# Mixers: the recurrence is prepared beside attention's end, its tree rows get the split input's space, branch products stand in the norm's waits, three barriers go

## The chip, the cores and the metric

One core of a Trainium2 chip runs the whole program as one launch. The metric is the device time of that launch in microseconds (us), the median of the executions. All arithmetic is float32. The products against the token mixers' wide inputs are split into a high and a low part.

## What is computed

The reference runs two blocks on 256 tokens of width 1024. The change concerns the first block, which has two layers. In each, a token mixer stands between two gated feed-forward parts:

```python
def token_mixer(h, w_in, pool_w, pool_scale, rel_bias, lb, norm_g, w_branch, w_out):
    proj = h @ w_in
    (a, q, k, v, qi, ki, wi, hq, hf, hi, hg, gates) = jnp.split(proj, MIX_SPLITS, axis=-1)
    y_a = pool_mixer(a, pool_w, pool_scale)
    y_b = sparse_attention(q, k, v, qi, ki, wi, rel_bias)      # top 64 of 256 keys, 4 heads
    y_c = hgrn2(hq, hf, hi, hg, lb, norm_g)                    # gated recurrence, 4 heads, then an RMS norm
    g = jax.nn.sigmoid(gates.reshape(B, S, 3, D_MODEL))
    merged = (g[:, :, 0] * (y_a @ w_branch[:256]) + g[:, :, 1] * (y_b @ w_branch[256:512])
              + g[:, :, 2] * (y_c @ w_branch[512:]))
    return merged @ w_out
```

The recurrence `hgrn2` is computed as a binary tree over tokens: for each of eight levels the prefix and suffix sums of the log decays (`pref`, `suff`) are exponentiated, multiplied with keys and queries into `treeX`, and multiplied with each other on TensorE.

## The kernel before

Every engine has its own program, written out by hand, and semaphores join them. Weights stream from memory as panels of 1 MB (256 output columns) into four slots (`slots`). SyncE issues them in order: the load of panel p waits until the panel four places before it has been multiplied. Products of a panel go to one of four banks (`accs`), and `acc_open` waits until the bank's last user was read. Four more banks (`mix`) hold everything small. Where a phase is named in `CARRY`, VectorE also weighs a 1 MB panel of another part in each step (`cond_weigh`), and SyncE waits for `cond_done` before it loads the next of these. In the branch phase of layer 0 there are three, in layer 1 none; in the output phase (`mixout`) four in either layer, those of layer 1 with twice the work.

A mixer runs in this order: 15 input panels; the pool; attention, with gate panels 2 to 6 in TensorE's waits; the recurrence (`hgrn`), with gate panels 7 to 11 in its waits; the branch products, 4 panels u in three parts r each (`ymix` rows 0-1 pool, 2-3 attention, 4-7 recurrence), whose results VectorE multiplies with the gates and adds into `merged`; and `mixout`, 4 panels that multiply `merged`. Between the phases stands a barrier of TensorE, VectorE and ScalarE:

```python
        def stage_end(eng, count):
            count[0] += 1
            eng.drain().then_inc(stage, 1)
            eng.wait_ge(stage, 3 * count[0])
```

Names: `hg_key` says that the keys and the first `pref` are made, `hg_x` that a level's rows are ready, `hg_mm` that its products are done, `hg_o` that the recurrence's output stands in `mix`, `hg_sq` that ScalarE squared it, `hg_ms` that TensorE summed the squares, `hg_inverse` that the inverse roots are there, which TensorE then spreads (`spread`) for the last product of VectorE into `ymix[:, 4:8]`. `probT_ready` and `attn_mm` belong to attention: transposed probabilities copied out, and the product with the values done.

Space: the scratch region at `TMP` is shared. Attention's `logit` lies in `TMP + 2816` and on, over the `treeX` and `pairs` of the recurrence. `sums` (the tensor `decay_sums`, 4 rows of 1024) holds the split input (`mix_hi`, `mix_lo`) during the 15 input panels and nothing from then on until the second block.

In the profile, L678 is a gate or mixout panel (32 matmul records a panel; one float32 matmul is two records), L923 the transposes, L933 the product with the values, L957 to L966 the tree's products, L975 to L977 the output's, L982 the sums of squares, L853 the spread, L1358 the branch products, L480 the barrier. L76, L81, L86, L91, L96 and L116 are the helpers that record every ScalarE and VectorE operation, L2144 a weighing.

## Time and profile before

| | |
|---|---|
| median of 3 executions | 2945.57 us (2941.25 to 2946.78) |
| the profiled execution | 2941.72 us, of which the span is 2939.7 us |
| TensorE busy | 2711.7 us, 92% of the span |
| VectorE, ScalarE, GpSimd busy | 1943.9, 1091.0, 238.7 us |
| granted TensorE clock, mean | 0.977 |
| memory read | 465.58 MB, 159 GB/s over the span |

TensorE is close to always busy, so what counts are the stretches where it waits or where its granted clock is below 1. All times below are microseconds from the span's start. The mixer of layer 0 ends its input panels near 351, and that of layer 1 near 1078.

### The profile page before, as it was taken

How to read it: one execution, taken by the hardware profiler on the slowest of the kernel's cores; microseconds unless marked ns; L12 is line 12 of the kernel's file. 1: busy time of each engine (PE TensorE's matmuls, PEld its weight loads, DVE VectorE, ACT ScalarE, POOL GpSimd, SP SyncE). 2: the span in 40 equal slices, each digit the busy share in tenths (PEclk: the TensorE clock that was granted, in tenths of full speed). 3: DMA queues.
4: the chain of work that ended last, by engine and by line, in shares of the span. 5: the costliest groups of instructions: out<-in, count | busy, mean ns of one | idle time of the engine just before them, and what ended most of it. 6: DMA issues, size and time to landing. Idle time of an engine off the chain costs nothing.

```text
span 2939.7 us, 48614 instructions
## 1 busy us (share of the span) xinstructions
PE 2711.7 (92%) x18294; PEld 2306.4 (78%) x18294; DVE 1943.9 (66%) x3303; ACT 1091.0 (37%) x1389; POOL 238.7 (8%) x135
## 2 busy tenths in 40 slices
PE   3999998999999999999989978999999899889998
PEld 3998977899998887799967854687744777667887
DVE  6776665777777766476746473577787676664881
ACT  2434432443542433154464542433300644542211
POOL 0000000000000000000012300244300000000000
PEclk9999999999999999999999989999999999999999
DMA  8775734677575553345512200222277221113442
GB/s 309 271 289 220 263 113 178 219 275 287 214 272 226 193 192 104 130 172 211 204 61 78 81 21 29 72 94 92 107 266 292 76 73 67 58 58 127 146 169 74
DMA packets 106384, 469.15 MB, mean 160 GB/s; under 512 B 7052, under 2 KB 57304, under 8 KB 58328
## 3 DMA queue, kind: packets, MB, share of 16 engines
q1 hardware_dynamic: 106200, 466.67, 43.8%
q8 instruction: 119, 1.95, 0.3%
q14 instruction: 65, 0.53, 0.1%
HBM read 465.58 MB, written 1.06 MB: 159 GB/s over the span
## 4 chain that ended last, share of the span: by engine, by line
PE 31%; DVE 12%; DVEq 7%; ACT 3%; issue 3%; DMA 2%; ACTq 1%; SPq 0%
DVEq L2859 4%; PE accs L830 4%; PE accs L693 3%; PE accs L678 3%; PE accs L694 3%; PE accs L695 3%; DVE arena L2836 3%; PE accs L1225 2%; PE accs L1226 2%; PE accs L1227 2%; DVE arena L2144 1%; DMA cond_panel<-wc 1%; PE accs L1358 1%; ACT arena L76 1%; DMA arena<-wc 1%
## 5 line engine op out<-in xcount | busy, mean ns | idle before, releaser
L693 PE MATMUL accs<-normed_r,arena_r 128*128 128x256 f32 (+2 forms) x1864 | 585.5, 314 | 17.2 <-DVEq L2189 6.3
L694 PE MATMUL accs<-arena_r 128*128 128x256 f32 x2069 | 585.8, 283 | 0.0
L695 PE MATMUL accs<-normed_r,panel_r 128*128 128x256 f32 (+2 forms) x1872 | 584.7, 312 | 0.0
L86 DVE TENSOR_TENSOR panel_r<-panel,arena_r 128x1024 fp32r<-128x1024 f32 (+1 forms) x295 | 390.6, 1324 | 162.7 <-ACTq L1507 117.7
L1506 ACT ACTIVATE arena_r<-panel 128x1024 fp32r<-128x1024 f32 (+1 forms) x292 | 330.5, 1132 | 328.8 <-DMA panel<-w 138.8
L693 PEld LDWEIGHTS accs<-normed_r,arena_r 128*128 128x128 f32 (+1 forms) x1864 | 350.4, 188 | 54.2 <-issue 14.0
L694 PEld LDWEIGHTS accs<-arena_r 128*128 128x128 f32 x2069 | 390.9, 189 | 1.1 <-issue 0.2
L695 PEld LDWEIGHTS accs<-normed_r,panel_r 128*128 128x128 f32 (+1 forms) x1872 | 350.2, 187 | 23.9 <-issue 0.8
L678 PE MATMUL accs<-normed,panel 128*128 128x256 f32 x1536 | 344.3, 384 | 6.7 <-ACTq L480 3.0
L2836 DVE SCALAR_TENSOR_TENSOR arena<-accs,vectors,arena 128x189 f32<-128x189 f32 (+2 forms) x704 | 279.3, 428 | 95.3 <-issue 65.4
L678 PEld LDWEIGHTS accs<-normed,panel 128*128 128x128 f32 x1536 | 291.7, 192 | 54.1 <-issue 4.6
L830 PE MATMUL accs<-arena,panel 128*128 128x256 f32 (+1 forms) x832 | 255.5, 469 | 2.0 <-DVEq L2744 0.8
L830 PEld LDWEIGHTS accs<-arena,panel 128*128 128x128 f32 x832 | 157.8, 190 | 99.2 <-issue 86.8
L76 ACT ACTIVATE arena<-accs 128x512 f32<-128x512 f32 (+2 forms) x128 | 75.3, 588 | 370.4 <-PE accs L695 232.4
L693 PE MATMUL accs<-arena_r 128*128 128x256 f32 x704 | 201.2, 286 | 10.7 <-DVEq L2189 10.7
L695 PE MATMUL accs<-arena_r,panel_r 128*128 128x256 f32 x704 | 199.7, 284 | 0.0
L1435 POOL TENSOR_TENSOR panel_r<-panel,arena_r 128x1024 fp32r<-128x1024 f32 x70 | 169.0, 2414 | 333.9 <-ACTq L1514 333.0
L76 ACT ACTIVATE arena<-arena 128x512 f32<-128x512 f32 (+7 forms) x108 | 97.5, 903 | 161.0 <-DVEq L2782 58.6
L1513 ACT ACTIVATE arena_r<-panel 128x1024 fp32r<-128x1024 f32 x72 | 76.3, 1060 | 204.0 <-PE accs L695 188.3
L91 DVE SCALAR_TENSOR_TENSOR residual<-accs,mods,residual 128x256 f32<-128x256 f32 x96 | 46.4, 483 | 156.0 <-PE accs L830 76.0
L76 ACT ACTIVATE arena<-residual 128x512 f32<-128x512 f32 (+1 forms) x56 | 31.9, 569 | 317.0 <-DVEq L2889 268.9
L693 PEld LDWEIGHTS accs<-arena_r 128*128 128x128 f32 x704 | 134.8, 192 | 12.5 <-issue 7.0
(417 smaller groups left out, 4714.6 us busy)
## 6 DMA issues: line engine op xcount, KB each, us to landing
panel<-w SPq DMA_DIRECT2D x250, 1024.0 KB, 4.9
panel<-w SPq DMA_DIRECT2D x48, 1408.0 KB, 8.0
cond_panel<-wc SPq DMA_DIRECT2D x57, 1024.0 KB, 6.3
normed<-wc SPq DMA_DIRECT2D x43, 1024.0 KB, 6.5
arena<-wc SPq DMA_DIRECT2D x19, 1024.0 KB, 4.9
residual<-xs SPq DMA_DIRECT2D x2, 1024.0 KB, 9.7
residual<-wc SPq DMA_DIRECT2D x1, 1024.0 KB, 12.0
residual<-crows SPq DMA_DIRECT2D x2, 512.0 KB, 9.4
```

What stands on the lines that cost most here:

```text
L76: i = self.eng.activation(*a, **k)
L86: i = self.eng.tensor_tensor(*a, **k)
L678: mm = pe.matmul(acc[b][:, o:o + ntok], w[:, k * PANEL + j * P:k * PANEL + j * P + P], rhs(k), start=(k == 0), stop=(k == KD - 1))
L693: pe.matmul(out, hi[:, k, 0:m], src_hi(k), start=clear and k == 0, stop=False, skip_group_check=True)
L694: pe.matmul(out, hi[:, k, 0:m], src_lo(k), start=False, stop=False, skip_group_check=True)
L695: mm = pe.matmul(out, lo[:, k, 0:m], src_hi(k), start=False, stop=last and k == n - 1, skip_group_check=True)
L830: mm = pe.matmul(acc[a % BANKS][:, o:o + ntok], w[:, k * PANEL + j * P:k * PANEL + j * P + P], src(part * kper + k), start=first, stop=(pa ...
L1435: pool.tensor_tensor(lo, half_panel(g, u, j), hi, ALU.subtract)
L1506: act.eng.activation(split_parts(g, u, j)[0], half_panel(g, u, j), ACT.Copy)
L1513: act.eng.activation(split_parts(g, u, j)[0], half_panel(g, u, j), ACT.Copy)
L2836: dve.eng.scalar_tensor_tensor(out=out, in0=src, scalar=scale, in1=out, op0=ALU.mult, op1=ALU.add)
L2859: dve.drain()
```

## The change

- The tree's rows (`pref`, `suff`, `treeX`) move from the scratch region to `sums`, so they no longer overlap attention's `logit`.
- The barriers between attention and recurrence, recurrence and branch, and branch and mixout go. Their place is taken by waits on `attn_mm` (VectorE, before the memset of `pairs`, which still overlaps attention's space), `ymix_early` and `ymix_late` (TensorE, for the attention rows and the recurrence rows of `ymix`) and `merged` (TensorE, before each second k of mixout's first panel).
- Gate panel 7 moves ahead of attention's product with the values, gate panel 11 ahead of the recurrence's output products.
- ScalarE's copy of attention's result moves from the end of attention to behind the first level's exponentials, together with the read of gate panel 7.
- Three of the twelve branch parts are multiplied earlier: (0,0) before the sums of squares, (0,1) behind them, (1,0) behind the spread.

```diff
-        pref, suff = region(TMP, 4 * T), region(TMP + 1024, 4 * T)
-        treeX = [region(TMP + 2048 + 1024 * i, 4 * T) for i in range(2)]
+        pref, suff = sums[:, 0, :], sums[:, 1, :]
+        treeX = [sums[:, 2 + i, :] for i in range(2)]
...
+                        if merge is not None and j == 0 and k % 2 == 0:
+                            pe.wait_ge(S("merged"), 4 * merge + k // 2 + 1)
...
                     mm.then_inc(S("probT_mm"), 1)
-                    if qb == 0:
-                        gate(l, 6)
+                    gate(l, 6 + qb)
...
             def hgrn(l):
                 k4, q4 = kk, qf
-                gate(l, 7)
...
+                gate(l, 11)
                 pe.wait_ge(S("hg_acc"), 7 * l + 7)
                 pe.wait_ge(S("hg_pairs"), l + 1)
...
                 mm.then_inc(S("hg_o"), 1)
-                gate(l, 11)
+                pe.wait_ge(S("ymix_early"), l + 1)
+                branch_part(l, 0, 0)
                 pe.wait_ge(S("hg_sq"), l + 1)
...
                 mm.then_inc(S("hg_ms"), 1)
+                branch_part(l, 0, 1)
                 pe.wait_ge(S("hg_inverse"), l + 1)
                 spread(0, 8).then_inc(S("hg_spread"), 1)
+                branch_part(l, 1, 0)
...
+            def branch_part(l, u, r):
+
+                g = G[f"branch{l}"]
+                ks = (range(0, 2), range(2, 4), range(4, 8))[r]
+                w = panel_in(g, 0, u)
+                b = acc_open(g, 0, u, r)
+                for j in range(2):
+                    for k in ks:
+                        mm = pe.matmul(acc[b][:, j * T:j * T + T], w[:, k * PANEL + j * P:k * PANEL + j * P + P],
+                                       ymix[:, k, :], start=(k == ks[0]), stop=(k == ks[-1]))
+                mm.then_inc(ready[b], 1)
...
                         attention(l)
-                        stage_end(pe, count)
                         hgrn(l)
-                        stage_end(pe, count)
-                        g = G[f"branch{l}"]
+                        pe.wait_ge(S("ymix_late"), l + 1)
                         for u in range(4):
...
+                            for r in range(3):
+                                if (u, r) not in ((0, 0), (0, 1), (1, 0)):
+                                    branch_part(l, u, r)
                         g = G[f"mixout{l}"]
                         for u in range(4):
-                            features(g, 0, u, lambda k: merged[:, k, :], T)
+                            features(g, 0, u, lambda k: merged[:, k, :], T, merge=l if u == 0 else None)
...
-                act.wait_ge(S("attn_mm"), l + 1)
-                act.activation(ymix[:, 2:4, :].rearrange("p a b -> p (a b)"), mix[:, 1, :], ACT.Copy)
...
-                    if lv in (1, 3, 5):
+                    if lv == 0:
+                        gate(l, 7)
+                        act.wait_ge(S("attn_mm"), l + 1)
+                        act.activation(ymix[:, 2:4, :].rearrange("p a b -> p (a b)"), mix[:, 1, :], ACT.Copy).then_inc(S("ymix_early"), 1)
+                    if lv in (3, 5):
                         gate(l, 7 + lv // 2)
...
-                dve.memset(pairs[:, :, :], 0.0)
...
+                    if lv == 0:
+                        dve.wait_ge(S("attn_mm"), l + 1)
+                        dve.memset(pairs[:, :, :], 0.0)
...
-                            dve.tensor_tensor(dst, dst, mtmp[:, :, :], ALU.add)
+                            i = dve.tensor_tensor(dst, dst, mtmp[:, :, :], ALU.add)
+                            if r == 2:
+                                i.then_inc(S("merged"), 1)
```

TensorE's program at attention's end, before (layer 0; L678 with `panel0` is gate panel 7):

```order
L923 MATMUL mix<-constants,arena 128x128 [waits prob_ready]
L923 MATMUL mix<-constants,arena 128x128 x7
L933 MATMUL mix<-arena 64x128 [waits probT_ready]
L933 MATMUL mix<-arena 64x128 x3
L933 MATMUL mix<-arena 64x128 [waits probT_ready]
L933 MATMUL mix<-arena 64x128 x7
L678 MATMUL accs<-normed,panel0 128x256 [waits acc_free0,panel_landed0,stage_end]
L678 MATMUL accs<-normed,panel0 128x256 x15
L957 MATMUL mix<-arena 32x32 [waits hg_key]
```

The same place now (the gate panel's line is L680, the product with the values L934):

```order
L925 MATMUL mix<-constants,arena 128x128 [waits prob_ready]
L925 MATMUL mix<-constants,arena 128x128 x7
L680 MATMUL accs<-normed,panel0 128x256 [waits acc_free0,panel_landed0]
L680 MATMUL accs<-normed,panel0 128x256 x15
L934 MATMUL mix<-arena 64x128 [waits probT_ready]
L934 MATMUL mix<-arena 64x128 x3
L934 MATMUL mix<-arena 64x128 [waits probT_ready]
L934 MATMUL mix<-arena 64x128 x7
L957 MATMUL mix<-arena 32x32 [waits hg_key]
```

The gate panel stands ahead of the product with the values, and no barrier is left between them and the tree.

TensorE's program between the recurrence's output and the branch products, before (layer 0):

```order
L678 MATMUL accs<-normed,panel0 128x256 [waits acc_free0,panel_landed0]
L678 MATMUL accs<-normed,panel0 128x256 x15
L982 MATMUL mix<-ones_h,arena 128x1 [waits hg_sq]
L982 MATMUL mix<-ones_h,arena 128x1 x7
L853 MATMUL mix<-constants,rms_columns 128x128 [waits hg_inverse]
L853 MATMUL mix<-constants,rms_columns 128x128 x7
L1358 MATMUL accs<-arena,panel1 128x256 [waits acc_free1,panel_landed1,stage_end]
L1358 MATMUL accs<-arena,panel1 128x256 x3
```

The same place now (L999 is `branch_part`):

```order
L999 MATMUL accs<-arena,panel1 128x256 [waits acc_free1,panel_landed1,ymix_early]
L999 MATMUL accs<-arena,panel1 128x256 x3
L984 MATMUL mix<-ones_h,arena 128x1 [waits hg_sq]
L984 MATMUL mix<-ones_h,arena 128x1 x7
L999 MATMUL accs<-arena,panel1 128x256 [waits acc_free2,panel_landed1]
L999 MATMUL accs<-arena,panel1 128x256 x3
L855 MATMUL mix<-constants,rms_columns 128x128 [waits hg_inverse]
L855 MATMUL mix<-constants,rms_columns 128x128 x7
L999 MATMUL accs<-arena,panel2 128x256 [waits acc_free0,panel_landed2]
L999 MATMUL accs<-arena,panel2 128x256 x3
L999 MATMUL accs<-arena,panel1 128x256 [waits acc_free3,panel_landed1,ymix_late]
```

Gate panel 11 has left this place (it now stands ahead of the output products), and three branch parts have come in between the three steps of the norm.

ScalarE's program from the end of attention to the second level, now (before, the copy `arena<-mix 128x512` stood ahead of the table load, and the table load waited for `hg_key`):

```order
L76 ACTIVATE arena<-mix 128x1024 [waits probT_mm]
L76 ACT_TABLE_LOAD
L76 ACTIVATE decay_sums<-decay_sums,constants 128x1024 [waits hg_key]
L76 ACT_TABLE_LOAD
L76 ACTIVATE decay_sums<-decay_sums 128x512 [waits hg_zero]
L76 ACTIVATE decay_sums<-decay_sums 128x512
L76 ACTIVATE arena<-accs 128x512 [waits acc_ready0]
L76 ACTIVATE arena<-mix 128x512 [waits attn_mm]
L76 ACTIVATE decay_sums<-decay_sums 128x256x2 [waits hg_sums]
```

The logarithm and the first exponentials stand directly behind the copy of the transposed probabilities; the read of gate panel 7 and the copy of attention's result stand behind them, ahead of the second level.

## Rows read from the trace of the kernel before

**Rows 1.** Timeline at attention's end, layer 0: start, duration, engine, line [idle before <-releaser]

```profile
410.76 1.04 PE L923 MATMUL mix<-constants,arena 128*128 128x128 f32 x8
...
411.83 1.02 ACT L76 ACTIVATE arena<-mix 128x1024 f32<-128x1024 f32 x1 [0.28 <-PE mix L923]
...
412.91 1.58 PE L933 MATMUL mix<-arena 128*64 128x128 f32 x16 [0.52 <-ACT arena L76]
...
415.23 1.65 DVE L81 TENSOR_SCALAR arena<-arena,one_minus_lb 128x256 f32<-128x256 f32 x4 [8.35 <-ACTq L480]
...
417.85 1.28 ACT L76 ACT_TABLE_LOAD   x1 [2.72 <-DVEq L2395]
```

**Rows 2.** Timeline, first levels of the tree, layer 0

```profile
423.14 1.51 DVE L86 TENSOR_TENSOR arena<-arena 128x512 f32<-128x512 f32 x2 [2.88 <-ACT arena L76]
...
424.77 1.47 ACT L76 ACTIVATE arena<-arena 128x512 f32<-128x512 f32 x2 [1.66 <-DVEq L2425]
...
426.42 0.76 PE L957 MATMUL mix<-arena 128*32 128x32 f32 x64 [3.30 <-DVEq L2428]
...
427.11 8.86 PE L678 MATMUL accs<-normed,panel 128*128 128x256 f32 x32
...
437.20 7.17 PE L678 MATMUL accs<-normed,panel 128*128 128x256 f32 x32
```

**Rows 3.** Timeline, end of the recurrence and its norm, layer 0

```profile
456.78 1.16 PE L966 MATMUL mix<-arena 128*128 128x128 f32 x8 [1.98 <-DVEq L2428]
...
465.42 1.02 ACT L76 ACTIVATE arena<-mix 128x1024 f32<-128x1024 f32 x1
...
467.78 2.17 DVE L91 SCALAR_TENSOR_TENSOR arena<-arena,vectors 128x256 f32<-128x256 f32 x4
...
469.85 1.84 PE L982 MATMUL mix<-ones_h,arena 128*128 128x1 f32 x16
...
472.91 2.05 PE L853 MATMUL mix<-constants,rms_columns 128*128 128x128 f32 x16 [1.23 <-DVEq L2438]
...
475.00 1.22 DVE L86 TENSOR_TENSOR arena<-arena,mix 128x1024 f32<-128x1024 f32 x1 [2.23 <-PE mix L853]
...
476.36 27.89 PE L1358 MATMUL accs<-arena,panel 128*128 128x256 f32 x128 [1.40 <-ACTq L480]
```

**Rows 4.** Timeline, VectorE and TensorE in the branch phase, layer 0

```profile
487.73 1.52 DVE L86 TENSOR_TENSOR arena<-accs,arena 128x512 f32<-128x512 f32 x2
...
494.62 1.52 DVE L86 TENSOR_TENSOR arena<-accs,arena 128x512 f32<-128x512 f32 x2
...
506.24 27.89 PE L678 MATMUL accs<-arena,panel 128*128 128x256 f32 x128 [1.99 <-DVEq L480]
```

**Rows 5.** Timeline, SyncE's loads in the branch phase, layer 0

```profile
487.67 0.58 SPq L563 DMA_DIRECT2D normed<-wc  x1
488.29 1.13 SPq L540 DMA_DIRECT2D panel<-w  x2
```

**Rows 6.** DMA issues from 488 to 492: KB each, median us to landing

```profile
panel<-w SPq DMA_DIRECT2D x2, 1024.0 KB, 8.5
```

**Rows 7.** Timeline, layer 1: transposes of attention, first panel of mixout

```profile
1134.02 1.04 PE L923 MATMUL mix<-constants,arena 128*128 128x128 f32 x8
...
1233.89 27.89 PE L678 MATMUL accs<-arena,panel 128*128 128x256 f32 x128 [1.74 <-DVEq L480]
```

**Rows 8.** Busy time by stage: stretch, us, busy of each engine (x), PEclk, DMA share, GB/s

```profile
427.10:437.20 10.10, 10.10 (x169) 8.44 (x161) 6.38 (x10) 1.70 (x3) 0.00 (x0) 0.83 0.07 12
...
1180.50:1202.80 22.30, 18.80 (x96) 17.27 (x96) 5.28 (x8) 11.76 (x12) 0.00 (x0) 0.76 0.15 55
```

**Rows 9.** TensorE alone in the output products of layer 1: us, busy (x), PEclk

```profile
1182.56:1187.63 5.07, 5.07 (x24) 0.50 0.00 0
```

**Rows 10.** All instructions of the second block on decay_sums: ns min/median/max, first and last start

```profile
L86 DVE TENSOR_TENSOR decay_sums<-decay_sums x32: 691/693/697, 1555.9 to 1654.6; 128x512 f32<-128x512 f32 x32
...
L2470 DVE MEMSET decay_sums<- x2: 912/912/912, 1543.6 to 1546.1; 128x1024 f32 x2
```

More of the change, by code:

```diff
@@ L663, in input_chunk, with features @@
                 pe.wait_ge(S("rms_out"), n * KD + k + 1)
-            def features(g, it, u, rhs, ntok, norm=None, js=range(2), h=None, used=False):
+            def features(g, it, u, rhs, ntok, norm=None, js=range(2), h=None, used=False, merge=None):
                 w = panel_in(g, it, u)
@@ L1971, in _ @@
                         attention(l)
-                        stage_end(act, count)
                         hgrn(l)
-                        stage_end(act, count)
-                        stage_end(act, count)
                         layer_norm(n, l, 1, G[f"mixout{l}"])
@@ L2440, in hgrn @@
                 dve.tensor_tensor(ymix[:, 4:8, :].rearrange("p a b -> p (a b)"), onorm[:, :, :].rearrange("p a b -> p (a b)"),
-                                  mix[:, 0:2, :].rearrange("p a b -> p (a b)"), ALU.mult)
+                                  mix[:, 0:2, :].rearrange("p a b -> p (a b)"), ALU.mult).then_inc(S("ymix_late"), 1)
             def branch(l):
@@ L2950, in _ @@
                         attention(l)
-                        stage_end(dve, count)
                         hgrn(l)
-                        stage_end(dve, count)
                         branch(l)
-                        stage_end(dve, count)
                         residual(G[f"mixout{l}"], l, 24 + 16, n)
```

9 lines of the change are left out of this document (removed).

## Prediction

> **What bounds the kernel now.** I read the table of the profile first: TensorE is busy 92% of the span, so time can only come from its waits and from stretches with a lower granted clock. Then I read the mixers in the timeline, layer by layer, looking on TensorE for "idle before" and for panels that take longer than others. Three things are to be seen.
>
> At attention's end [rows 1] the transposes are done at 411.80 (410.76 + 1.04) and ScalarE has copied them at 412.85. VectorE has been idle for 8.35 us when the barrier lets it go at 415.23: it was free at 406.88. Only then does it make the recurrence's keys (ScalarE waits 2.72 us for them before its table load at 417.85), and the first level follows so late that TensorE, after gate panel 7, waits 3.30 us [rows 2].
>
> The gate panel behind that wait takes 8.86 us where the next one takes 7.17 [rows 2]; the granted clock of that stretch is 0.83 [rows 8]. The same happens at the recurrence's end: 1.98 us of waiting before the last level [rows 3], then the output products, which in layer 1 run wholly at half clock, 24 records in 5.07 us [rows 9]. Layer 1 keeps 0.76 from there to the branch phase [rows 8].
>
> Behind the recurrence, TensorE waits for the norm and for two barriers: 1.23, 1.40 and, at mixout, 1.99 us [rows 3, 4].
>
> **The change on the path, layer 0.** TensorE starts at 411.80, where both kernels are alike.
>
> - Gate panel 7 follows at once: 7.17 [rows 2] to 418.97. The product with the values: its larger half is 16 records in 1.58 [rows 1], so 24 in about 2.3, to 421.3. First tree product 0.76 [rows 2], to 422.0.
> - The recurrence's preparation now starts at 406.88 on VectorE. It took from 415.23 to 417.85, so `hg_key` comes at about 409.5, ahead of ScalarE, which is free at 412.85. From ScalarE's table load to VectorE's first sum pass 5.29 us (417.85 to 423.14), from there to the next product 3.28 (to 426.42) [rows 1, 2]: `hg_x` at 412.95 + 8.57 = 421.5. TensorE, free at 422.0, no longer waits. Second product 0.76, to 422.8.
> - Gate panel 8 without the wait before it: 7.17, to 430.0. The two products behind it took 1.23 (435.97 to 437.20), so gate panel 9 starts at 431.2, not at 437.20: **6.0 us** gained.
> - The two moved ScalarE steps (panel 7's read, attention's copy) end at 422.0, after `attn_mm` at 421.3. Level 1 follows: exponentials 1.47, two pairs of VectorE operations 3.28 [rows 2]: 426.8. A take (256 elements; 0.6 with its gap, an estimate from 0.69 for 512 in rows 10) and level 2's pairs: 430.6. That is 0.6 behind gate panel 8, but there is one product (0.6) in between. So the moved steps cost nothing by a hair; each us more would be paid in full. VectorE's memset of `pairs` (0.91 [rows 10]) and its wait on `attn_mm` stand at 421.5 to 422.6, while VectorE would wait for these exponentials until 423.5. Only VectorE's take of level 0 and its level 1 stand behind it; it is covered, and would cost about 1.1 if it were not.
> - From gate panel 9 to the last level's start nothing changes: 437.20 to 456.78 are 19.58 [rows 2, 3], to 450.8; its products 1.16, to 452.0.
> - Gate panel 11 now comes here: 7.17, to 459.1. It covers ScalarE's copies and its long sigmoid. The output products follow a dense panel: 24 records at full clock are half of 5.07 [rows 9], 2.6, to 461.7.
> - Part (0,0): 8 of 128 records of 27.89 [rows 3], 1.74, to 463.5. ScalarE squares meanwhile, 1.02 [rows 3], to 462.8. Sums of squares 1.84 to 465.3, part (0,1) 1.74 to 467.1. VectorE's copy and four products took from the end of the square to 469.95, 3.5 [rows 3]: 466.3, and its reciprocal of eight columns some tenths, before 467.1. Spread 2.05 to 469.2, part (1,0) 1.74 to 470.9, which covers VectorE's last product (1.22). The other 104 records take 22.7 [rows 3]: 493.6.
> - Mixout's first panel needs `merged` of all four panels. VectorE now starts at 470.5 with three parts waiting, and needs 6.89 a panel, of which 0.4 was waiting for TensorE (487.73 to 494.62) [rows 4]: 6.5. Three panels with their weighing and 4.2 for the last end at 494.2 if it never waits, near 496 with the wait for part (0,2) at 474.3. The wait for the last rows stands six matmuls of 0.44 into the panel, at 496.2. It costs nothing, or some tenths.
> - One thing does become late. SyncE issues branch panel 3 only behind the load that waits for the first weighing [rows 5], and it took 8.5 us to land [rows 6]. The weighing ends at about 478.6 now, so the panel is there near 487.6; TensorE wants it at 486.7. I take **0.7 us** (0 to 1.5).
>
> Mixout starts at 494.3 instead of 506.24 [rows 4]: **11.9 us**. Mixout itself is unchanged, 27.89 in both layers [rows 4, 7]; VectorE's weighings there move with it.
>
> **Layer 1.** The same steps, 723.26 later (1134.02 against 410.76 [rows 1, 7]), without weighings and so without the late panel: 493.6 + 723.3 = 1216.9 instead of 1233.89 [rows 7]: **17.0 us**. It gains more because it lost more to the clock before [rows 8, 9].
>
> **The clock in the sum.** These 28.9 us hold for full clock throughout. But the wait of 1.98 us before the last level stays, and gate panel 11 stands behind it now. A fall costs what panel 8 shows, 8.86 - 7.17 = 1.7 [rows 2]. In layer 1 the clock fell behind that wait [rows 9]; now a dense panel follows at once. I take one fall for both layers: 27.2 us. The Trainium skill ("TensorE: Matmul & The Clock Gate", section "The HAM clock gate") says that half clock is the default state and that activity releases it. The trace agrees (0.83 behind the wait of 3.30 us); by the rule alone, with the waits filled and no fall, the sum would be 28.9 and the time 2916.7, inside the forecast's own band. It also speaks against counting on that, since a wait stays in just this place.
>
> The placement of the tree's rows I cost at nothing: a VectorE operation of 512 elements on that tensor takes 0.693 us [rows 10], and two of them on the old one take 1.51 with the gap between [rows 2]. The new semaphore increments and waits lie on drains that were there. No instruction of work is added; SyncE's order is the same.
>
> **The sum.** 2945.57 - 27.2 = **2918.4 us**. The profiled execution stood at 2941.72, 3.9 below the median; from it the same sum gives 2914.5. Nothing behind mixout can take the gain back that I see: the loads there wait for progress, not for a time.
>
> **The rivals.**
> - *The waits come back in part*: the clock falls in gate panels 8 and 11 of both layers (4 x 1.7, 5.1 more than taken), or level 2, which has no slack, comes 1 to 2 us late in each layer. For it: the tree's pace is set by the chain through ScalarE and VectorE, close to TensorE's in my working. Against: 3.30 us of wait are gone ahead of panel 8. Gain 18 to 25, time 2920.5 to 2927.5, about 2923.5. Chance 0.23.
> - *The branch tail gives half back*: VectorE, not TensorE, sets the end of the branch phase and panel 3 is late by several us, because three loads of 1 MB come in one burst. Then the early parts are worth nothing (3 x 1.74 in each layer, 10.4, and 2 more): gain near 15, 2931. Against: 6.5 a panel is under TensorE's 6.97 (27.89 / 4), and layer 1 has no weighings. 0.05.
> - *No change*: gains under 5.9 us. It would need the recurrence to keep its start, for instance because ScalarE's table load still waited for something late. 0.03.
> - *Slower*: the tree's operations take longer in the new tensor. Each level is a chain, so what 30 VectorE operations of 0.69 [rows 10] and 16 exponentials of 0.73 [rows 2] take more is paid in full. They sum to 32.4 us a layer; at 45% more the gain of 28.9 is gone, and with 60% more the time is about 2955. Against it stands the 0.693 of rows 10. 0.03.
> - *More than 31 us*: the drops of the clock elsewhere shrink as well. 0.07, near 2912.
>
> **How the numbers follow.** The forecast itself, gains of 25 to 31 or 2914.5 to 2920.5, has 0.59. The range 2912 to 2928 holds it, the first rival and most of the last. 0.2% of the time is 5.9 us, about what a measurement of this kernel can tell from no change. Faster 0.94, same 0.03, slower 0.03.
>
> **What the profile after would show.** Attention's product with the values directly ahead of the tree, no idle over 1 us on TensorE until the last level; a gate panel 8 of about 7.2 us; output products in 2.6 us in both layers; mixout's first panel near 494 and 1205 (1216.9 less layer 0's 11.9) from the start. Wrong would be: a wait of TensorE before the fourth product, a gate panel 11 of over 8 us, a wait for the branch's fourth panel of over 1.5 us, or tree operations on VectorE longer than 0.75 us.

## The result and the profile after

The changed kernel took 2910.67 us, median of 4 executions (2906.15 to 2913.43), against 2946.18 (2941.25 to 2954.94, 4 executions) for the kernel before beside it: ratio 0.9881 with a 95% interval of 0.9868 to 0.9894, some 35 us. It was forecast at 2918.4, 2912 to 2928. The sign and most of the mechanisms were right, the gain of 27.2 was too small by 4 to 8 us (three measurements, below). The profiled executions lie closer: 2913.43 against 2941.72, 28.3 us.

The page of the changed kernel, its span and busy times:

```profile
span 2911.6 us, 48608 instructions
PE 2697.7 (93%) x18294; PEld 2294.3 (79%) x18294; DVE 1943.9 (67%) x3303; ACT 1091.0 (37%) x1389; POOL 240.3 (8%) x135
```

The timeline of TensorE in layer 0, changed kernel (start, duration, operation, records, and in brackets idle time before and what ended it); it answers to [rows 2 to 4]:

```profile
414.29 1.04 PE L925 MATMUL mix<-constants,arena 128*128 128x128 f32 x8
415.16 7.07 PE L680 MATMUL accs<-normed,panel 128*128 128x256 f32 x32
422.17 2.02 PE L934 MATMUL mix<-arena 128*64 128x128 f32 x24
424.11 0.76 PE L957 MATMUL mix<-arena 128*32 128x32 f32 x64
424.99 0.76 PE L957 MATMUL mix<-decay_sums 128*32 128x32 f32 x64
425.68 7.17 PE L680 MATMUL accs<-normed,panel 128*128 128x256 f32 x32
...
434.43 0.76 PE L957 MATMUL mix<-decay_sums 128*32 128x32 f32 x64 [0.88 <-DVEq L2434]
435.12 7.17 PE L680 MATMUL accs<-normed,panel 128*128 128x256 f32 x32
...
454.38 1.16 PE L966 MATMUL mix<-decay_sums 128*128 128x128 f32 x8 [1.68 <-DVEq L2434]
455.38 7.07 PE L680 MATMUL accs<-normed,panel 128*128 128x256 f32 x32
...
464.97 1.89 PE L999 MATMUL accs<-arena,panel 128*128 128x256 f32 x8
466.69 1.84 PE L984 MATMUL mix<-ones_h,arena 128*128 128x1 f32 x16
468.40 1.97 PE L999 MATMUL accs<-arena,panel 128*128 128x256 f32 x8
470.21 1.96 PE L855 MATMUL mix<-constants,rms_columns 128*128 128x128 f32 x16
...
489.80 7.17 PE L999 MATMUL accs<-arena,panel 128*128 128x256 f32 x32 [0.36 <-DMA panel<-w]
496.81 3.40 PE L680 MATMUL accs<-arena,panel 128*128 128x256 f32 x15
```

From the eight transposes to the last level there are gate panels 7 to 10 and tree products with three waits: 0.88, 0.23 (not shown) and 1.68 us. Before, there were five in this place: 0.52, 3.30 and 1.98 [rows 1 to 3], 0.16 ahead of the sixth tree product, and the barrier's own:

```profile
415.25 7.17 PE L678 MATMUL accs<-normed,panel 128*128 128x256 f32 x32 [0.75 <-ACTq L480]
```

Behind the last level nothing waits any more until branch panel 3, whose load is 0.36 us late; gate panel 11, the output products (462.29 to 464.97) and the three early branch parts fill it. Mixout starts 82.52 us behind the eight transposes (414.29 to 496.81); before it was 95.48 [rows 1, 4].

Layer 1 of the same kernel, against [rows 7]:

```profile
1162.41 1.16 PE L966 MATMUL mix<-decay_sums 128*128 128x128 f32 x8 [1.68 <-DVEq L2434]
...
1204.20 2.11 PE L680 MATMUL accs<-arena,panel 128*128 128x256 f32 x9
```

Its transposes start at 1122.78, so this is 81.42 us against 99.87. The windows of the changed kernel (stretch, its length, TensorE's busy time, granted clock, DMA share, GB/s) show full clock over the whole stretch from attention's first transposes to the norm behind mixout in layer 0 and in layer 1, where [rows 8] had 0.83 and 0.76 in places:

```profile
406.89:524.44 117.55, 114.28 (x981) 1.00 0.52 196
1115.38:1231.83 116.45, 114.20 (x981) 1.00 0.45 163
```

**Where the 28.1 us between the two spans came from.** I cut both traces at the same instructions: at attention's first four transposes (403.36 before, 406.89 after) and at the first product of the norm behind mixout (533.97 and 524.44), and the same in layer 1. Call the two stretches between these marks "the mixers". They took 265.6 us before and 234.0 after: 31.6 less. A stretch between two norms in layer 0's feed-forward part, far from every edit (742.49 to 959.17 before), took 216.7 and then 213.4: 3.3 less. The rest is 6.8 more, 5.1 of it at the start of the program, which the change does not touch. So two numbers are to be explained: 31.6 where 27.2 were forecast, and 3.3 where nothing was; and beyond them, why the medians differ by more than these two executions.

### The profile page after: what moved, and what is told of

The parts are those of the page before. It is cut to its first block, busy times and chain, and to the rows that moved or that the text cites. A ratio compares the mean times of both kernels' runs of the same rounds, so it can differ in the third digit from the quotient of the medians.

```text
span 2911.6 us, 48608 instructions
## 1 busy us (share of the span) xinstructions
PE 2697.7 (93%) x18294; PEld 2294.3 (79%) x18294; DVE 1943.9 (67%) x3303; ACT 1091.0 (37%) x1389; POOL 240.3 (8%) x135
## 4 chain that ended last, share of the span: by engine, by line
PE 48%; DVE 24%; DVEq 9%; ACT 6%; DMA 6%; issue 5%; ACTq 1%; SPq 1%; POOLq 0%
PE accs L680 7%; PE accs L695 7%; PE accs L696 7%; PE accs L697 7%; DVE panel_r L86 5%; DVEq L2870 4%; PE accs L832 4%; DMA panel<-w 3%; DVE arena L2847 3%; DVE arena L2151 2%; PE accs L1241 2%; ACT arena L76 2%; PE accs L1242 2%; PE accs L1243 2%; DVE cond_panel L2151 2%
## 5 line engine op out<-in xcount | busy, mean ns | idle before, releaser
L680 PE MATMUL accs<-normed,panel 128*128 128x256 f32 x1536 | 340.5, 381 | 5.2 <-ACT normed L76 2.4
L680 PEld LDWEIGHTS accs<-normed,panel 128*128 128x128 f32 x1536 | 288.8, 190 | 51.2 <-issue 4.9
L697 PEld LDWEIGHTS accs<-arena_r,panel_r 128*128 128x128 f32 x704 | 133.1, 189 | 0.0
```

The costliest lines, as they stand in the source:

```text
L680: mm = pe.matmul(acc[b][:, o:o + ntok], w[:, k * PANEL + j * P:k * PANEL + j * P + P], rhs(k), start=(k == 0), stop=(k == KD - 1))
L697: mm = pe.matmul(out, lo[:, k, 0:m], src_hi(k), start=False, stop=last and k == n - 1, skip_group_check=True)
```

## Experiments

The times of experiments come from three chips: the first four kernels on one, the next four on another, the last four on a third. Beside each time stands "mixers", the sum of the two stretches from that kernel's own trace, because it is not touched by what the start of the program does from one execution to the next.

**The changed kernel once more**, to see which of the two surprises stays.

> The changed kernel once more, in more rounds against the kernel before. Theory A: the gain is what its trace shows inside the mixers, from attention's transposes to the norm behind mixout: 130.61 - 117.55 = 13.1 us in layer 0 and 135.00 - 116.45 = 18.6 us in layer 1, together 31.6 us, and nothing elsewhere; the ratio is then near 0.9893 (gain 29 to 33). Theory B: the change also speeds up something outside the mixers, as the medians (35.5 us) suggest; the ratio stays near 0.9880 and a stretch outside the mixers is shorter in this profile too.

2915.16 us (2913.86 to 2919.64) against 2946.89 (17 executions, 2939.31 to 2955.23), ratio 0.9895 [0.9874, 0.9916], 31.7 us by the medians. Mixers 235.8. The far stretch took 213.4 again: the ratio is the one of theory A, and yet a part outside the mixers is shorter, as theory B had it. One clock fall appeared that the first trace did not have, behind the last level's wait in layer 0 (timeline of this run):

```profile
455.05 2.08 PE L966 MATMUL mix<-decay_sums 128*128 128x128 f32 x8 [1.68 <-DVEq L2434]
456.92 7.84 PE L680 MATMUL accs<-normed,panel 128*128 128x256 f32 x32
```

The wait of 1.68 us is the same; the records behind it take 2.08 and 7.84 instead of 1.16 and 7.07, and the spread comes 1.6 us later behind the last level (17.5 for 15.8). This is the fall that the prediction had counted once over both layers. It comes in some executions and not in others.

**The front half alone**: the recurrence is prepared beside attention's end, the tree's rows lie in the new place; the order behind the last level and the two barriers around the branch are as before.

```
-                gate(l, 11)            (behind the last level)
                 ...output products...
+                gate(l, 11)
-                branch_part(l, 0, 0)   (and (0, 1), (1, 0): back in the branch loop)
                         hgrn(l)
+                        stage_end(pe, count)
                         ...12 branch parts...
+                        stage_end(pe, count)
```

> The front half alone: tree rows in the split input's space, the barrier between attention and recurrence gone, gate panel 7 and the copies moved. Gate panel 11, the branch parts and the other two barriers stand as before. Theory A (the halves are independent): gate panel 9 starts 5.6 and 6.6 us earlier in the two layers and all behind it keeps its length, clock falls included: gain 12 to 13 us. Rival B: the time gained in front is partly lost behind, since the tree's levels meet TensorE sooner: gain under 9 us.

2926.32 us, ratio 0.9933 [0.9917, 0.995], some 21 us where theory A had 12 to 13 and rival B under 9. Mixers 252.1. That is 13.5 less than in the first trace of the kernel before (265.6), from which theory A was read and which it fits, and 17.8 less than in the mean of three traces.

**The back half alone**: gate panel 7, both copies and the memset stand where they stood, with the barrier behind attention; everything behind the last level is as in the changed kernel.

```
-                    gate(l, 6 + qb)
+                    if qb == 0:
+                        gate(l, 6)
                         attention(l)
+                        stage_end(pe, count)
                         hgrn(l)
```

> The back half alone: gate panel 11 ahead of the output products, three branch parts in the norm's waits, the barriers around the branch phase gone; attention's end and the start of the recurrence as before (the tree's rows stay in their new place). From the last level's start to mixout the trace of before has 49.5 and 53.4 us, that of after 42.4 and 41.8. Theory A: gain 7.0 + 11.6 = 18.6 us (17 to 20), gate panel 8 still at 8.9 us. Rival B: the clock stays up at the recurrence's end only because the front half is dense too; then the output products run at half clock and the gain is under 15 us.

2926.14 us, ratio 0.9928 [0.9911, 0.9945], some 21 us (theory A: 17 to 20). Mixers 249.4. The timeline shows the old wait, the old slow panel 8, and a new slow panel 11, while the output products behind it run at full clock (466.52 to 469.20), against rival B:

```profile
426.91 1.08 PE L959 MATMUL mix<-decay_sums 128*32 128x32 f32 x64 [3.33 <-DVEq L2437]
427.92 8.21 PE L680 MATMUL accs<-normed,panel 128*128 128x256 f32 x32
...
456.95 1.72 PE L968 MATMUL mix<-decay_sums 128*128 128x128 f32 x8 [1.98 <-DVEq L2437]
458.46 8.22 PE L680 MATMUL accs<-normed,panel 128*128 128x256 f32 x32
```

Either half gives 21 us; the whole gave 32 beside them. The three intervals are 9.7, 10.0 and 12.4 us wide, so the times don't say whether 10 us are had by either half. The mixers say that it is less: against the mean of three traces of the kernel before (269.9, below) the halves gain 17.8 and 20.5, in sum 38.3, and the whole 35.3. So, as far as one trace of each can say, the halves are of about the same worth and nearly additive.

**The kernel before with its two longest waits filled** by products whose results are not used: 12 before the second tree product, 8 before the last level. The waits stay for everybody else; only TensorE is kept busy. This prices the clock alone.

```
                     else:
+                        busy({1: 12, 8: 8}.get(i, 0))
                         pe.wait_ge(S("hg_x"), 8 * l + i)
```

> The kernel before with nothing of the change, but 12 idle 128-column products in TensorE's wait ahead of the second tree product and 8 in the wait ahead of the last level (2.8 and 1.9 us, about as long as the waits). The waits and barriers stay; what the idle time did to the clock goes. Theory A (a good part of the gain was clock): gate panel 8 falls from 8.86 to 7.2 us in both layers and the output products from 4.1 and 5.2 to 2.7: gain 6 to 8 us. Rival B (the falls have another cause): panel 8 stays at 8.9, gain 0 or a small loss.

2944.29 us, ratio 0.9988 [0.9977, 0.9999], 3.5 us (0.3 to 6.8), under the 6 to 8 of theory A, though both falls that it names are gone. Mixers 258.6. The profiled execution was the slowest of twelve (2950.74 us), with 2690.1 us outside the mixers where the kernel before has 2672.8 to 2675.8. Its timeline:

```profile
435.15 7.17 PE L678 MATMUL accs<-normed,panel 128*128 128x256 f32 x32
...
463.14 1.16 PE L967 MATMUL mix<-arena 128*128 128x128 f32 x8
...
467.95 7.07 PE L678 MATMUL accs<-normed,panel 128*128 128x256 f32 x32
...
477.93 3.50 PE L853 MATMUL mix<-constants,rms_columns 128*128 128x128 f32 x16 [1.23 <-DVEq L2439]
```

Gate panel 8 takes 7.17 instead of 8.86 [rows 2] and panel 11 comes 4.8 us behind the last level, not 6.2 [rows 3]. The spread takes 3.50 where [rows 3] had 2.05, but that is no fall moved here by the filling: in the other two traces of the kernel before, and in layer 1 of the first, the spread takes 3.17 to 3.79 with nothing filled. In the mixers TensorE is busy for 243.6 us, of which the 80 added records are 10.0. Its own records take 233.6, where the kernel before has 245.2 in the mean of three traces and the changed kernel 229.0 (below): by this one trace, the two places hold some 11.6 of the 16.2 us that the clock costs. The rest is not shorter: 15.0 us of idle time and the 10.0 of added records are about the 24.6 of before.

**Gate panel 11 back behind the output products**, all else as changed.

```
-                gate(l, 11)
                 pe.wait_ge(S("hg_acc"), 7 * l + 7)
                 ...output products...
+                gate(l, 11)
                 pe.wait_ge(S("ymix_early"), l + 1)
```

> The changed kernel with gate panel 11 back behind the recurrence's output products (ahead of branch part (0,0)). Theory A: TensorE waits about 1 us for the pairs, the output products fall to half clock again (4.1 to 5.2 us instead of 2.7): 3 to 4 us a layer, the kernel is 6 to 9 us slower than the changed one, gain over before near 24. Rival B: the order of the panel and the products is neutral, since both are TensorE work: under 3 us slower than the changed kernel.

2915.38 us against 2946.85, ratio 0.9894 [0.988, 0.9907]. Mixers 240.6. In the timeline of layer 0 the output products start at 451.90, after a wait of 0.87 us, and run at about half clock: panel 11 starts at 456.31, 6.44 us behind the last level. In the changed kernel panel 11 and the output products together take 9.59 behind the last level's product (455.38 to 464.97), in this one 6.44 - 1.00 + 6.91 = 12.35. That is 2.8 us in layer 0; with layer 1 the mixers are 5 to 7 us longer. The time does not show it: 2915.4 cannot be told from the 2915.2 and 2914.9 of the changed kernel's repeats, on other chips. The ratio's interval is 7.9 us wide, so the times exclude neither 0 nor the 5 to 7 us of the mixers, and the 6 to 9 us of theory A are not confirmed.

**No early branch parts**: all twelve parts stand behind the norm, as before; the barriers stay away.

```
-                pe.wait_ge(S("ymix_early"), l + 1)
-                branch_part(l, 0, 0)
...
-                branch_part(l, 0, 1)
...
-                branch_part(l, 1, 0)
```

> The changed kernel with no branch part in the norm's waits: all twelve stand behind the wait for the last rows of ymix. The three barriers stay away. Theory A: the waits for the square, the inverse roots and VectorE's last product come back, 1.1 + 2 + 1.4 = 4 to 5 us a layer, and some clock: 8 to 12 us slower than the changed kernel. Rival B: VectorE sets the end of the branch phase, as the second rival of the prediction has it, so early parts are worth little: under 4 us slower.

2925.56 us, ratio 0.9932 [0.992, 0.9944]: 10 us above the changed kernel's repeats, inside theory A's 8 to 12. Mixers 250.4, 16 more. Its timeline:

```profile
451.43 1.92 PE L966 MATMUL mix<-decay_sums 128*128 128x128 f32 x8 [1.68 <-DVEq L2430]
453.15 8.01 PE L680 MATMUL accs<-normed,panel 128*128 128x256 f32 x32
...
464.95 1.95 PE L982 MATMUL mix<-ones_h,arena 128*128 128x1 f32 x16 [1.11 <-ACT arena L76]
468.81 3.61 PE L855 MATMUL mix<-constants,rms_columns 128*128 128x128 f32 x16 [1.92 <-DVEq L2443]
473.78 27.86 PE L995 MATMUL accs<-arena,panel 128*128 128x256 f32 x128 [1.36 <-issue]
```

The norm's three waits are back, 4.39 us in one layer, and the spread loses 1.7 more to the clock; layer 1 is as much longer (125.2 for 116.5). Of the 16 us, 8 are idle time (13.6 for 5.5). The rest is slower records, and some of these, as the 1.92 and 8.01 above, stand ahead of the edit: they belong to this execution and not surely to the parts. The parts bring no work that had to be done additionally: they are the same 24 records, laid where TensorE stood still.

**The barrier between branch and mixout back**, all else as changed.

```
                                     branch_part(l, u, r)
+                        stage_end(pe, count)
```

> The changed kernel with the barrier between the branch phase and mixout back. Theory A: TensorE waits for VectorE's last merge, 2.4 us in layer 0 (VectorE ends at 499.2, mixout started at 496.8) and 1.8 in layer 1: about 4 us slower than the changed kernel. Rival B: mixout would wait for merged anyway, and the barrier costs under 1 us.

2915.49 us, ratio 0.9899 [0.9886, 0.9913]. Mixers 240.7. The timeline has the wait:

```profile
498.33 4.13 PE L680 MATMUL accs<-arena,panel 128*128 128x256 f32 x12 [2.34 <-DVEq L480]
```

The wait of 2.34 us is paid at once, and mixout took 29.6 instead of 27.9 in layer 0. Again the trace sees 6 us and the time sees none of the 4 that theory A had.

**The late copies and the late load moved**: ScalarE's two moved steps one level later, VectorE's memset at the fourth level, branch panel 3 of layer 0 issued ahead of the weighing's load (its lines are left out below). This asks whether the 0.88 us before the fourth tree product and the 0.36 before branch panel 3 are worth having.

```
-                    if lv == 0:
+                    if lv == 1:
                         gate(l, 7)
...
-                    if lv == 0:
+                    if lv == 3:
                         dve.wait_ge(S("attn_mm"), l + 1)
                         dve.memset(pairs[:, :, :], 0.0)
```

> A version meant to be better: ScalarE's two copies move behind the second level's exponentials, VectorE's memset of pairs to the fourth level, and in layer 0 the fourth branch panel is loaded ahead of the weighing panel that waits. Theory A: the waits of 0.88 and 0.21 us ahead of the fourth tree product and of 0.36 us for the branch panel go: 1 to 2 us faster than the changed kernel, which its profile shows and its time hardly. Rival B: the chain through ScalarE and VectorE gets no shorter, because the products behind the gate panel set it: no wait changes.

2913.43 us, ratio 0.989 [0.9873, 0.9906], which can't be told from the changed kernel. Mixers 235.7, no gain where theory A had 1 to 2 us. Both waits are gone and others stand in their place, since the memset of 0.91 us holds up the chain at the fourth level as it did at the first:

```profile
442.64 0.76 PE L960 MATMUL mix<-decay_sums 128*32 128x32 f32 x64 [1.40 <-DVEq L2437]
...
454.19 1.16 PE L969 MATMUL mix<-decay_sums 128*128 128x128 f32 x8 [1.98 <-DVEq L2437]
```

**The kernel before, profiled twice more**, to see whether its profiled execution was typical.

> The kernel before once more, one look. In its first trace the stretch between the norm behind the first block's fourth feed-forward part and the next one (742.49 to 959.17) took 216.68 us; in the six kernels with the change or a part of it it took 212.9 to 213.4, and in the one with idle products only 214.9. Theory A: this is chance of one execution (a wait for a panel and a clock fall behind it, 0.91 to 0.96 in the last 60 us): the stretch takes anything from 213 to 217 here. Theory B: the change moves the loads there to a better phase, and the stretch takes 216 to 217 in every execution of the kernel before: 3 us of the gain are then made outside the mixers.

> The kernel before a third time, one look, for the same question: by theory A (chance) the three looks differ by 2 us or more in that stretch, by theory B they agree within 1 us at 216 to 217.

2947.15 and 2949.39 us, spans 2945.1 and 2947.4 where the first trace had 2939.7; mixers 269.3 and 274.7 where it had 265.6. The far stretch took 216.5 and 215.6: three traces within 1.1 us, which speaks for theory B. The rows of the third trace (layer 0) show where the mixers differ:

```profile
475.57 3.24 PE L853 MATMUL mix<-constants,rms_columns 128*128 128x128 f32 x16 [1.23 <-DVEq L2438]
480.20 30.95 PE L1358 MATMUL accs<-arena,panel 128*128 128x256 f32 x128 [1.40 <-ACTq L480]
513.14 29.58 PE L678 MATMUL accs<-arena,panel 128*128 128x256 f32 x128 [1.98 <-DVEq L480]
```

The waits are those of [rows 3, 4] within a hundredth: 1.23, 1.40, 1.98. Behind them the spread takes 3.24 instead of 2.05, the branch 30.95 instead of 27.89, mixout 29.58 instead of 27.89: the clock fell behind each. In the first trace of layer 0 it fell behind none of these three; in the second the spread took 3.79 and the branch 29.99. Layer 1's branch took 29.34, 27.89 and 30.95 in the three traces.

**A version beyond both**: the late copies moved as above, but the memset at the third level just ahead of its take, and gate panel 11 cut in two, half of it into the wait before the last level and half behind.

```
                     bank = 2 * (i % 2)
+                    if i == 8:
+                        features(G[f"gate{l}"], 0, 11, lambda k: H[:, k, lat], T, js=(0,))
...
-                gate(l, 11)
+                features(G[f"gate{l}"], 0, 11, lambda k: H[:, k, lat], T, js=(1,))
```

> A version meant to be better: the late copies, with VectorE's memset of pairs at the third level instead of the fourth, where it made a wait of 1.4 us ahead of the sixth tree product, the fourth branch panel loaded earlier, and gate panel 11 in two halves, one ahead of the last level's wait and one behind its products. Theory A (TensorE's work sets the time, so each wait that is filled counts): the waits of 0.9 and 0.2 us before the fourth tree product, of 1.7 us before the last level in both layers and of 0.4 us for the branch panel go, and no clock falls there: 4 to 5 us faster than the changed kernel. Rival B: ScalarE's sigmoid, which ends only now in time, becomes late for the square: under 2 us faster, with a wait of TensorE ahead of the sums of squares.

> The changed kernel a third time, beside the version with half panels on the same chip. Theory A: gain 31.6 us if the clock stays up behind the last level's wait, 1.7 less for each layer where it falls: ratio 0.989 to 0.990. Rival B (the first measurement's 0.9881 is the usual one): gain 35 us.

2906.01 us (2904.82 to 2909.48), ratio 0.9865 [0.984, 0.989]; the changed kernel beside it on the same chip 2914.95 (2913.53 to 2915.57), ratio 0.9891 [0.9866, 0.9915]. The two ranges do not touch: 9 us faster than the changed kernel here. (In its first measurement the changed kernel had 2906.15 to 2913.43, which does touch.) Mixers 229.0 against 233.9. Timeline, layer 0:

```profile
450.33 3.72 PE L683 MATMUL accs<-normed,panel 128*128 128x256 f32 x16
```

The half panel of 3.72 us stands where TensorE waited 1.68, the last level follows without a wait, and no wait over 0.2 us is left in the recurrence. The two half panels cost 0.1 us more than the whole one (3.56 and 3.46 from start to start, against 6.91), so the gain is the waits themselves: the changed kernel's were 0.88 + 0.23 + 1.68 + 0.36 in layer 0 and 0.21 + 0.22 + 1.68 in layer 1, 5.3 in sum; 0.16 is left in each layer, which makes 4.9, and the mixers gained 4.9, inside theory A's 4 to 5; no wait stands ahead of the sums of squares, against rival B. The changed kernel's own gain in this measurement, 33.6 us, lies between its two theories. The other 4 us of the time lie outside the mixers and are not explained.

## Why the prediction was right, and where it was wrong

Shift the prediction's times of layer 0 by 3.53 us, since its eight transposes stood at 410.76 and those of the changed kernel at 414.29.

- **Gate panel 7 and attention's product.** Forecast: the first tree product at 424.8; it came at 424.11. Right, and the 0.7 us is the first part of a size that was off. I added record durations, 7.17 and 2.3. But the profile lets a group's last record end after the next group has started: 415.16 to 422.17 are 7.01, 422.17 to 424.11 are 1.94.
- **No wait before the second product.** Right: the fourth row of the timeline is followed by the fifth with none, where there were 3.30 us.
- **Gate panel 8 at 7.2.** Right: 7.17 in layer 0 in all three traces of the changed kernel, 7.31 to 7.36 in layer 1.
- **Gate panel 9 at 434.7** (431.2 + 3.53). It came at 435.12, 0.4 late, as the first two steps were early and level 2 was late.
- **"The moved steps cost nothing by a hair."** Wrong by 0.88 us in layer 0 (0.81 and 0.87 in the other two traces of the changed kernel) and 0.21 in layer 1. A wait before the fourth product was one of the signs of being wrong that the prediction named. VectorE's own timeline of layer 0 shows which step:

```profile
421.72 1.51 DVE L86 TENSOR_TENSOR decay_sums<-decay_sums 128x512 f32<-128x512 f32 x2 [7.45 <-ACT decay_sums L76]
...
425.27 0.91 DVE L116 MEMSET arena<- 128x1024 f32 x1 [0.41 <-issue]
426.25 0.42 DVE L86 TENSOR_TENSOR arena<-mix,constants 128x256 f32<-128x256 f32 x1
...
432.84 1.46 DVE L86 TENSOR_TENSOR decay_sums<-decay_sums,arena 128x512 f32<-128x512 f32 x2 [0.66 <-issue]
```

  The memset and its gap hold the take back to 426.25, where 0.17 us of gap were usual. I had set it beside a wait for exponentials until 427.0 (423.5 + 3.53); these end at 426.37, so it is not wholly covered and costs some 0.4. A gap of 0.66 instead of 0.17 at 432.84 adds 0.5, in layer 0 of all three traces of this kernel and not in layer 1; its cause stays open. The level's operands were ready at 434.30, close to the 434.1 forecast; TensorE came for them 0.6 earlier than I had it.
- **The tree's rows in the new place at no cost.** Right: two operations take 1.51 and 1.46 in the new tensor, as in the old one [rows 2]. The rival that ends slower hung on this and is excluded.
- **From gate panel 9 to the last level 19.58.** Measured 19.26 (435.12 to 454.38).
- **Gate panel 11 and the output products at full clock, 2.6.** Right: 462.29 to 464.97 are 2.68, in layer 1 1170.31 to 1172.99 the same. With panel 11 behind them instead, layer 0's took 4.4 (451.90 to 456.31).
- **Parts in the norm's waits.** Right, to 0.1 us each: the spread was forecast at 470.6 and came at 470.21. Without them the mixers are 16 us longer, the time 10.
- **Late branch panel 3: 0.7 (0 to 1.5).** Right in kind, 0.36, none in layer 1. Its load is issued at 482.12, 7.7 us ahead of its use, where I had 8.5 to landing [rows 6].
- **`merged` costs mixout nothing, or some tenths.** Right: its 128 records start at 496.81 and run without a wait in either layer, in 27.79 us.
- **One clock fall for both layers, 1.7.** Inside what happens, but not in this trace: none in the first and third, one (1.6) in the second.
- **The sum per layer.** 11.9 was 12.96, 17.0 was 18.45. With the 1.7 for a fall, 1.1 + 1.5 + 1.7 = 4.2 of the 4.4 us that the mixers gained beyond 27.2.

**The step that failed** is the sum: "2945.57 - 27.2". It set a gain read from one execution against the median of all. So it compared the spread, the branch phase and mixout ("Mixout itself is unchanged") at the clock that they happened to have in that execution. The term was 27.2; the mixers gained 31.6 us in the first pair of traces and 35.3 in the mean of three.

*The kernel before loses more to the clock than its profile showed.* Its mixers took 265.6, 269.3 and 274.7 in three traces, 269.9 in the mean; those of the changed kernel 234.0, 235.8 and 233.9, in the mean 234.6. The windows of TensorE over the two mixers (stretch, its length, busy time, granted clock, DMA share, GB/s) say where the difference lies. The kernel before, first trace and third:

```profile
403.36:533.97 130.61, 118.41 (x980) 0.97 0.48 177
1126.62:1261.62 135.00, 122.58 (x980) 0.94 0.39 140
...
404.50:542.55 138.05, 125.85 (x980) 0.91 0.45 168
1134.46:1271.08 136.62, 124.18 (x981) 0.93 0.39 139
```

The idle time, length less busy, is 24.6 us in all three traces of the kernel before, and 5.5, 5.7 and 5.4 in those of the changed one: the waits are worth 19.1 us, whatever the execution. The busy time of the same work (1960 to 1962 records) is 241.0, 244.7 and 250.0 before, and 228.5, 230.1 and 228.5 after: slower records are worth 12.5 us in the first pair and 16.2 in the mean. These 3.7 us more are what one trace could not show. The times agree: over the 17 executions of the kernel before on one chip the mean granted clock goes from 0.978 in the fastest (2939.31 us) to 0.973 in the slowest (2955.23). The profiled execution was the best of the three, which its time, 3.9 us under the median, could have told: I wrote down both 2918.4 and, from that execution itself, 2914.5, and took the sum from the median as if the 3.9 were spread over the program. Removing a wait takes away not only its length but also the chance of a fall behind it.

*Three us are gained far away, and lost again elsewhere.* The stretch from 742.49 to 959.17 took 216.7, 216.5 and 215.6 before, and 213.4, 213.4 and 213.2 in the changed kernel, 212.9 to 213.7 over the experiments that start from it; the two groups do not touch. Its last 60 us, before:

```profile
900.00:940.00 40.00, 34.54 (x271) 0.96 0.74 286
940.00:959.20 19.20, 17.34 (x133) 0.91 0.32 110
```

and the changed kernel in the same work:

```profile
890.40:930.40 40.00, 33.52 (x276) 1.00 0.77 289
930.40:946.30 15.90, 15.82 (x133) 1.00 0.35 126
```

The granted clock is 1.00 where it was 0.96 and 0.91, but the clock is not the whole cause: in the second trace of the changed kernel it fell there too (0.91 over 20 us), and the stretch still took 213.4. What differs in every trace stands ahead of it, a load of 1408 KB that is issued 157 us into the stretch (898.99 before, 889.79 after). The rows of the DMA issues, before and in the changed kernel (KB each, us to landing):

```profile
panel<-w SPq DMA_DIRECT2D x1, 1408.0 KB, 10.0
...
panel<-w SPq DMA_DIRECT2D x1, 1408.0 KB, 8.6
```

It took 10.0, 9.8 and 10.1 us to land in the three traces of the kernel before, and 8.4 to 8.8 in all that start from the changed one. TensorE's wait for what is made of it was 3.55, 3.35 and 3.62 us against 1.8 to 2.2. No instruction there was changed. The kernel before with its waits filled, which keeps its barriers, has the early landing (8.6) and the short wait (2.1), with a clock fall in the last 40 us, and took 214.9, between the groups. Why the load lands later in the kernel before was not found.

These 3 us cannot be added to the gain. All that lies outside the mixers, this stretch included, took 2674.1, 2675.8 and 2672.8 us before and 2677.6, 2677.3 and 2679.3 in the changed kernel, 3.9 more in the mean. So the spans of the three and three traces differ by 35.3 less 3.9, 31.4 us in the mean. That is near the gains of the two repeats (31.7 and 33.6). The 35.5 of the first measurement is more; its profiled execution, 2913.43, was the slowest of its four, so no trace shows where the rest was gained. No run shows why the part outside the mixers is longer; in the experiments that start from the changed kernel it is 2669.3 to 2675.9.

The forecast named this: "the drops of the clock elsewhere shrink as well", near 2912, at 0.07. It was the case that came, and had too little, though the drops that shrank stood in the mixers for the most part. Two of the three medians (2915.16 and 2914.95) fell inside the range and the first 1.3 us under its end. In the three measurements the gain was 35.5, 31.7 and 33.6, against a forecast of 27.2.

**What is not settled.** Single edits worth 6 us in the mixers of one trace (panel 11 behind the output products, the barrier at mixout) did not show in the time at all. The parts of a program outside the mixers vary between executions (its start took 243.2 to 250.1 us over all traces, without regard to the kernel), and one trace of each is too little to add the parts up to the time. No repeat of the changed kernel was run on the chip of these experiments, so they stand against its times on other chips.

## What to carry to other kernels

A wait on TensorE costs its length and, behind it, a chance of slower records: price both, look at the kernel before in more than one execution before taking its clock for granted, and ask where its profiled time stands to its median. Fill waits with dense work of the same program, in pieces as small as the wait (a panel cut in halves cost 0.1 us extra): filling with empty work won back the clock behind the wait (11.6 us in the traces, 3.5 in the time) but none of the waits. The same small instruction in a chain may be paid at one place and free at another: the memset of 0.91 us cost some 0.4 us of a wait at the first level and a wait of 1.40 at the fourth, and nothing at the third.

## What the hardware showed that I had not expected

- The same wait in the same kernel is followed by a fall of the clock in one execution and not in another. The barrier of 1.40 us ahead of the branch phase is followed by 27.89, 29.99 and 30.95 us for the same 128 records in layer 0; 1.68 us ahead of the last level by 1.16 and 2.08 us for 8 records. In the execution with 2.08 us, the changed kernel's second, the granted clock is 0.83 between 452 and 462 us, so a part of that stretch ran at 1.2 instead of 2.4 GHz. The Trainium skill ("TensorE: Matmul & The Clock Gate", section "The HAM clock gate") says that throttling is the default and activity releases it; the traces agree (each fall named in this text stands behind a wait), and show besides that behind the same wait of 1.2 to 2.0 us one execution has a fall and the next has none.
- A change in one part of a program shortened another, unchanged part that begins 200 us later by 3 us in 217, in every trace: one load of 1408 KB there lands after 8.4 to 8.8 us where it took 9.8 to 10.1, and the clock falls less behind it.
- ScalarE's table load stands in the changed kernel's timeline with 1.28 us at 416.45, and the next exponential starts at 417.75. The Trainium skill ("ScalarE: Activation LUTs", section "What ACT_TABLE_LOAD costs") gives about 1.28 us for the load, which agrees, and about as much again for a drain, of which nothing is to be seen here: 0.02 us lie between.
- Record durations overlap. A panel of 32 records reads 7.07 or 7.17 and the next group starts 7.01 or 7.11 later (415.16 to 422.17, 425.68 to 432.79); a group of 8 reads 1.16 and the next starts 1.00 later. From the eight transposes to the output products, fifteen groups, that adds up to 1.0 us, in one direction.
